# Second-product weights loaded through ScalarE's queue

## What is computed

```python
def swiglu(x, w_in, w_out):
    gu = x @ w_in
    g, u = jnp.split(gu, 2, axis=-1)
    return (jax.nn.silu(g) * u) @ w_out

x = x + 0.5 * swiglu(rmsnorm(x, norm_ffn1), ffn1_w_in, ffn1_w_out)
...
x = x + 0.5 * swiglu(rmsnorm(x, norm_ffn2), ffn2_w_in, ffn2_w_out)
```

## Time and profile before

| | us |
|---|---|
| median of 3 runs | 2199.1 |
| the profiled execution | 2206.41 |
| its span, first to last instruction | 2204.5 |
| TensorE busy (9208 matmuls) | 2084.3, 95% |
| VectorE busy | 1389.5, 63% |
| GpSimd busy | 891.9, 40% |
| ScalarE busy | 744.9, 34% |
| granted TensorE clock, mean | 0.968 |

### The profile page before, as it was taken

One profiled execution on the slowest core, in us unless ns is written; L12 is line 12 of the kernel. 1 busy time (PEld: TensorE's weight loads), 2 busy tenths in 40 slices (PEclk: granted clock), 3 DMA queues, 4 the chain that ended last, 5 costly groups with the idle time before them and its releaser, 6 DMA issues. The chain is left out here.

```text
span 2204.5 us, 27577 instructions
## 1 busy us (share of the span) xinstructions
PE 2084.3 (95%) x9208; PEld 1692.4 (77%) x9208; DVE 1389.5 (63%) x1570; ACT 744.9 (34%) x1048; POOL 891.9 (40%) x604
## 2 busy tenths in 40 slices
PE   7899999978898899999999999998999999888997
PEld 6688888866777788888877768886888888666776
DVE  5888887855445625434755555457888888655444
ACT  5444444421113321221134444224444444321112
POOL 0344444446568412312211112351444444366664
PEclk8999999989999999999999999999999999999998
DMA  3334344587652311112111114331544444695541
GB/s 115 126 130 166 133 171 143 186 307 273 246 209 76 115 59 41 57 57 76 58 48 39 53 58 151 129 143 45 175 142 157 147 166 148 244 348 199 201 171 76
DMA packets 147910, 307.85 MB, mean 140 GB/s; under 512 B 14096, under 2 KB 28560, under 8 KB 147856
## 3 DMA queue, kind: packets, MB, share of 16 engines
q1 hardware_dynamic: 139648, 278.97, 36.5%
q10 hardware_dynamic: 8208, 28.21, 3.4%
HBM read 205.42 MB, written 101.71 MB: 139 GB/s over the span
## 5 line engine op out<-in xcount | busy, mean ns | idle before, releaser
L1493 DVE SCALAR_TENSOR_TENSOR x<-ps,x 128x512 f32<-128x512 f32 x336 | 231.8, 691 | 235.6 <-PE ps L589 232.7
L1839 POOL TENSOR_TENSOR w_lo<-stage,w_hi 128x1024 fp32r<-128x1024 f32 x55 | 145.1, 2638 | 423.6 <-ACT w_hi L928 423.6
L537 PE MATMUL ps<-a_hi,w_hi 128*128 128x512 f32 x752 | 252.9, 404 | 1.2 <-DVE a_lo L1787 0.7
L537 PE MATMUL ps<-a_hi,w_lo 128*128 128x512 f32 x752 | 242.4, 390 | 0.0
L537 PE MATMUL ps<-a_lo,w_hi 128*128 128x512 f32 x752 | 242.3, 389 | 0.0
L1854 POOL TENSOR_TENSOR gb<-gb,rstd 128x512 f32<-128x512 f32 x42 | 89.4, 2130 | 353.4 <-DVE gb L1414 353.4
L1899 POOL TENSOR_TENSOR lo<-st,hi 128x1024 fp32r<-128x1024 f32 (+1 forms) x92 | 178.1, 1958 | 41.9 <-ACT hi L1029 41.9
L1029 ACT ACTIVATE hi<-st 128x1024 fp32r<-128x1024 f32 (+1 forms) x48 | 47.4, 988 | 386.8 <-POOL st L1890 256.4
L589 PE MATMUL ps<-a_hi,hi 128*128 128x512 f32 x264 | 113.1, 428 | 59.5 <-POOL lo L1899 37.9
L537 PEld LDWEIGHTS ps<-a_hi,w_lo 128*128 128x128 f32 x752 | 141.2, 188 | 29.8
L537 PEld LDWEIGHTS ps<-a_lo,w_hi 128*128 128x128 f32 x752 | 141.4, 188 | 29.4
(11 more groups left out here) (268 smaller groups left out, 4772.8 us busy)
## 6 DMA issues: line engine op xcount, KB each, us to landing
stage<-wstream SPq DMA_DIRECT2D x56, 512.0 KB, 3.3
b_spill<-raw_lo SPq DMA_DIRECT2D x110, 256.0 KB, 2.6
b_spill<-bh_a SPq DMA_DIRECT2D x88, 256.0 KB, 4.2
st_a<-win SPq DMA_DIRECT2D x42, 512.0 KB, 3.9
st_b<-win SPq DMA_DIRECT2D x42, 512.0 KB, 4.5
st<-wout SPq DMA_DIRECT2D x80, 256.0 KB, 3.9
b_spill<-bh_b SPq DMA_DIRECT2D x66, 256.0 KB, 4.0
t_hi<-b_spill SPq DMA_DIRECT2D x24, 512.0 KB, 10.1
```

Source lines behind the costliest of these rows:

```text
L537: mm = pe.matmul(ps[:, bank, :], w[0:r, k, :], mv[0:r, k, HALF * half:HALF * half + HALF], start=first and part == 0, stop=final and part ...
L1493: dve.scalar_tensor_tensor(out=x[:, m, part], in0=ps[:, bank, :], scalar=0.5, in1=x[:, m, part], op0=ALU.mult, op1=ALU.add).then_inc(xacc, 1)
L1839: pool.tensor_tensor(w_lo[:, parity, :, :], stage[:, parity, :, :], f32(w_hi[:, parity, :, :]), ALU.subtract).then_inc(wlo_done, 1)
```

## The change

`load_w2` moves from SyncE's program into ScalarE's, and is issued by ScalarE's queue. A helper `next_w2(f, s)` waits for the low part of pass s and then loads pass s + 2; it stands behind `high2(f, s)` for each s from 2 to 21. The pair of pass 0 stands in front of `high2(f, 0)` in the last `pair_in`; that of pass 1 behind the last silu, and right behind it that of pass 2; that of pass 3 stands behind the last `rest_combos`, in front of `high2(f, 2)`.

```diff
--- before.py
+++ after.py
@@ -411,19 +411,6 @@
                                  b_spill[qs[0]:qs[-1] + 1, NPROD * h + r, :, :].rearrange("q p n -> p q n")
                                  ).then_inc(cmb_first[r] if c == 0 else cmb_loaded[CMB_OF[c]], 16)
 
-            def load_w2(f, s):
-                b = s % 2
-                if s >= 2:
-                    sp.wait_ge(lo2_done, 2 * (NS * f + s - 1))
-                if kt_of(s) == 1:
-                    src = wodd[4 * f + s % 4, :, :].rearrange("p (s n) -> p s n", s=4)
-                    dst = st2[b][:, :, 0, :]
-                else:
-                    src = wout[(NS - 4) * f + (s if s < 4 else s - 4), :, :].rearrange("p (s n) -> p s n", s=4)
-                    dst = st2[b].rearrange("p s k n -> p s (k n)")
-                sp.dma_start(dst[:, 0:2, :], src[:, 0:2, :]).then_inc(w2_loaded[b], 16)
-                sp.dma_start(dst[:, 4:7:2, :], src[:, 2:4, :]).then_inc(w2_loaded[b], 16)
-
             def ffn(f):
                 J0, S0 = NP * f, NS * f
                 sp.wait_ge(lo1, 4 * J0 + 2)
@@ -445,21 +432,14 @@
                 last = J0 + NP
                 for r in range(NPROD):
                     sp.wait_ge(prod1, NPROD * (last - 1) + r + 1)
-                    if r == 6:
-                        load_w2(f, 1)
                     load_combo(f, 0, r, *CHUNKS[0])
                     if r == 1:
                         sp.wait_ge(c11_done, last)
                         reload_x(f, 1)
-                    if r == 3:
-                        load_w2(f, 0)
-                load_w2(f, 2)
                 sp.wait_ge(b1_done, last)
                 for m in (2, 6):
                     reload_x(f, m)
                 for r in range(NPROD):
-                    if r == 4:
-                        load_w2(f, 3)
                     load_combo(f, 1, r, *CHUNKS[1])
                 store_rest(f, (None, NQ - 1))
                 for r in (0, 2, 4, 1, 5):
@@ -468,13 +448,9 @@
                     reload_x(f, m)
                 for r in range(NPROD):
                     load_combo(f, 2, r, CHUNKS[2][0][:1], CHUNKS[2][1][:1])
-                load_w2(f, 4)
-                load_w2(f, 5)
                 for r in range(NPROD):
                     sp.wait_ge(prod2, NPROD * (S0 + 3) + r + 1)
                     load_combo(f, 2, r, CHUNKS[2][0][1:], CHUNKS[2][1][1:])
-                for s in range(6, 10):
-                    load_w2(f, s)
                 for c in range(3, len(CHUNKS)):
                     for r in range(NPROD):
                         sp.wait_ge(prod2, NPROD * (S0 + 4 * c - 5) + r + 1)
@@ -484,10 +460,6 @@
                         else:
                             load_combo(f, c, r, qs[:1], ks[:1])
                             load_combo(f, c, r, qs[1:], ks[1:])
-                    for s in range(4 * c - 2, 4 * c + 2):
-                        load_w2(f, s)
-                load_w2(f, NS - 2)
-                load_w2(f, NS - 1)
 
             load_w(U_TAIL1, 1, first=True)
             load_x(XO[0])
@@ -1016,6 +988,21 @@
                     act.wait_ge(b_stored[r], was_stored(Q, r, 0))
                     combo_high(r)
 
+            def load_w2(f, s):
+                b = s % 2
+                if kt_of(s) == 1:
+                    src = wodd[4 * f + s % 4, :, :].rearrange("p (s n) -> p s n", s=4)
+                    dst = st2[b][:, :, 0, :]
+                else:
+                    src = wout[(NS - 4) * f + (s if s < 4 else s - 4), :, :].rearrange("p (s n) -> p s n", s=4)
+                    dst = st2[b].rearrange("p s k n -> p s (k n)")
+                act.dma_start(dst[:, 0:2, :], src[:, 0:2, :]).then_inc(w2_loaded[b], 16)
+                act.dma_start(dst[:, 4:7:2, :], src[:, 2:4, :]).then_inc(w2_loaded[b], 16)
+
+            def next_w2(f, s):
+                act.wait_ge(lo2_done, 2 * (NS * f + s + 1))
+                load_w2(f, s + 2)
+
             def high2(f, s):
                 b, S = s % 2, NS * f + s
                 kt = kt_of(s)
@@ -1051,6 +1038,8 @@
                 if more:
                     next_weights(J, 1)
                 else:
+                    load_w2(last_of, 0)
+                if not more:
                     high2(last_of, 0)
                 silu_second(J)
 
@@ -1067,12 +1056,16 @@
                 last = NP * (f + 1)
                 J, Q = (None, last), (None, NQ * (f + 1) - 1)
                 silu_first(J)
+                load_w2(f, 1)
+                next_w2(f, 0)
                 rest_combos(J, Q, 0)
                 high2(f, 1)
                 rest_combos(J, Q, 1)
                 rest_combos(J, Q, 2)
+                next_w2(f, 1)
                 for s in range(2, NS - 2):
                     high2(f, s)
+                    next_w2(f, s)
                 end = NPROD * NS * (f + 1)
                 high2(f, NS - 2)
                 for t in range(2):
```

## The result

| | before | after |
|---|---|---|
| median, us | 2200.02 (4 runs) | 2148.92 (4 runs) |
| ratio, 95% interval | | 0.9771 (0.9754 to 0.9788) |
| span of the profiled run | 2204.5 | 2146.7 |
| its granted TensorE clock | 0.968 | 0.983 |

The change takes 51.1 us off. 2144 was predicted, with a range of 2130 to 2165: a gain of 55.4 us, 4.3 more than came.

The account below looks back on a forecast made before the run. TensorE was busy 95% of the span, so only its idle and low-clock time could be won. Gaps 53.6 plus start 1.8 make 55.4 us: 2206.4 to 2151.0 profiled, 2144 us for the median, range 2130 to 2165.

Parts of the forecast that it names:

- Part 1, the gaps: Before passes 4, 10, 14 and 18 of both blocks: earlier issue by ScalarE closes all eight gaps, gaining 53.6 us.
- The length of a pair in a backlog: Two `wout` loads on ScalarE's queue beside SyncE's backlog: 4.1 us for packets plus 2.3 latency, 6.4 us a pair.
- Part 2, the start: Passes 0 to 2: GpSimd starts 1.8 us earlier, two ScalarE issues cost 0.9; net gain 0.9 a block, 1.8 both.
- Part 3 and 4: ScalarE's 96 issues at 0.45 us, 43 us, fit its idle time; SyncE's freed queue wins nothing.
- signs of being right: No L1899 wait over 1 us from pass 3, passes 9.53 and 6.1, clock 1.00, pairs 5 to 7, pass 2 within 2.
- signs of being wrong: Pairs at 13 us or more, ScalarE issues above 1.5, GpSimd idle before pass 10, TensorE waiting for chunk loads or x.
- The high end of the range: Whole kernel: both starts 6.7 us later, 2159, plus a third of ScalarE's price: 2165 us.
- ScalarE's price: Slow issues on ScalarE, up to 2.51 us each, make passes late: some 18 us a block lost.
- A starved queue: Rival, at the start: pairs take up to 26 us beside SyncE's full queue, gaps stay, 2230 us; 5%.
- ScalarE pays for the issue: Rival, ScalarE's passes: issues up to 2.51 us each lose some 18 us a block, 2181 us; 7%.
- Nothing lands sooner: Rival, pairs in the backlog: they land behind it whoever issues, gaps stay, 0.9 us a block added, 2201 us; 3%.

Follow-up runs that it names:

- e8: Kernel before, with only the pairs from pass 4 on moved to ScalarE's queue, pairs 0 to 3 left on SyncE's: 2146.9 us, 0.9762.
- e1: Kernel before, all loads still in SyncE's queue, pairs for passes 4, 10, 14 and 18 moved ahead among the chunk loads: 2160.6 us, 0.9828.
- e2: Changed kernel, pairs for passes 10, 14 and 18 issued on ScalarE's queue about 7 us later than they could be: 2165.8 us, 0.9856.
- e5: Changed kernel, SyncE holds back all but the first of chunk 0's seven combinations until pass 0's pair has landed: 2147.6 us, 0.9757.
- e10: Changed kernel once more, unedited, run as a repeat on the same chip as a later version: 2153.0 us, 0.9778.

## Why the prediction was right, point by point

**Part 1, the gaps (53.6 us).** Right in mechanism and size: 26.52 + 27.12 = 53.6 us in passes 4 to 20. e8 shows that this part alone is the whole gain. e1 and e2 show that it has two halves: the time of issue, which alone all but closes the gaps before passes 10, 14 and 18, and the own queue, which alone narrows them. They overlap, and are not two sums to be added. The idle gap and the slow clock behind it were rightly priced together, by whole passes.

**The length of a pair in a backlog (6.4 us).** Too short. The pairs of passes 0 and 1 in the changed kernel, by ScalarE's issues and the first sums of VectorE and GpSimd:

```profile
448.66 0.60 ACT L974 ACTIVATE gb<-ps 128x512 f32<-128x512 f32 x1 [2.12 <-PE ps L561]
448.67 0.40 ACTq L999 DMA_DIRECT2D st<-wout  x1
...
464.74 0.34 ACTq L999 DMA_DIRECT2D st<-wout  x1
...
457.71 0.43 DVE L1441 TENSOR_TENSOR st<-st 128x256 f32<-128x256 f32 x1 [5.63 <-DMA st<-wout]
...
472.89 0.74 POOL L1880 TENSOR_TENSOR st<-st 128x256 f32<-128x256 f32 x1 [6.15 <-DMA st<-wout]
```

9.0 and 8.2 us. The pair of pass 10 took 9.8, here by ScalarE's issue and by GpSimd:

```profile
536.07 0.35 ACTq L999 DMA_DIRECT2D st<-wout  x1
...
545.88 0.74 POOL L1880 TENSOR_TENSOR st<-st 128x256 f32<-128x256 f32 x1 [2.16 <-DMA st<-wout]
```

The DMA view of the changed kernel shows what the model left out, for pass 0's pair, issued at 448.67. First from 448.67 to 452.25, then from 452.25 to 457.25:

```profile
q1 hardware_dynamic: 696, 1.34, 102.0%
```

```profile
q1 hardware_dynamic: 598, 1.40, 73.0%
q10 hardware_dynamic: 416, 0.52, 31.2%
```

In the first 3.6 us not one packet of ScalarE's queue was served. Then all 416 of the pair took 5.0 us, and VectorE began 0.5 us later. The model had 4.1 us for the packets, so one packet in turn was nearly right. The Trainium skill (DMA: Bandwidth & Descriptors, Queues, rings and completion order) says that a DMA engine goes round its queues packet by packet; the trace agrees, with 488 packets to 502 in e2. Too short was the fixed part: 2.3 us, where 3.6 + 0.5 passed. It came from loads alone on the wires, and there the first packet of a pair follows 1.0 us after the issue (677.23 and 678.2 in the kernel before). Why it takes 3.6 us beside a backlog stays open; e2 has 3.7 us for it (546.04 and 549.75), and e5, with hardly any backlog, 1.9. Besides, the 3.0 and 9.8 us that the prediction reads the earlier trace rows are medians of single transfers; the pairs took 3.5 us alone and 11.7 before pass 10. The error hardly mattered, as passes from 4 on had 13 us.

**Part 2, the start (a gain of 1.8 us).** This is the term that failed: it became a loss of 1.25 + 0.42 us. By its own formula, with two pairs of 9.0 and 8.2 us in the place of two of 6.4, GpSimd's first sum comes 2.6 us late and a forecast 1.8 - 0.9 = 0.9 a block turns into a loss of 3.5. It came out milder for three reasons. Pass 0's pair was issued with the start of the copy and not behind its end (448.67 for 449.3), and pass 1's with the start of the last silu (464.74 for 465.4), so GpSimd's first sum came 1.3 us late, counted from the copy, and not 2.6. The two issues cost about 0.5 us on ScalarE and not 0.9. And in f = 0 one of GpSimd's next sums (L1890, now L1883) took 0.73 us for 1.20, which no run explains.

**Part 3 and 4.** ScalarE's 96 issues took 0.33 to 0.73 us each, and from pass 3 on TensorE waited for no high half, as said. SyncE's freed queue gave nothing, as said.

**Not foreseen:** 0.74 us in passes 21 to 23 of f = 0 and 0.37 in pass 3 of f = 1, both of which the sum had at nothing. Their cause stays open; they are of the size by which one profile differs from the next (passes 21 to 23 of f = 0 take 37.2 us in e10, the same kernel).

**The signs.** Most signs of being right came: no wait for GpSimd's low line from pass 3 on, 9.52 and 6.1 us a pass, clock 1.00, pass 2 within 2 us of its place. One did not, the pair in 5 to 7 us. Two signs of being wrong came as well, both too small to matter: GpSimd stood idle for 2.2 us on a transfer of `wout` before pass 10, which TensorE did not feel, and TensorE waited 0.7 and 0.5 us for chunk 0's loads.

**The high end of the range.** It adds 6 us as a third of ScalarE's price. That price was 18 us a block, 36 in all, so a third is 12 us and the end 2171.

**The rivals.** A starved queue: no, 8 to 10 us and not 26. ScalarE pays for the issue: no. Nothing lands sooner: no. The Trainium skill's sentence that issuing from several engines saves only issue time (the same page, Issuing engines are not separate DMA queues) does not hold here as it stands. An earlier issue is worth three quarters of the gain, by e1, but e2 shows that the own queue saves more than issue time: 8.1 for 11.7 us at the same moment of issue.

## What to carry to other kernels

When a small load is late, look at two times apart: when its place was free and when it was issued, and then how long it took against its length alone. Here 7.6 us were its place in a hand-written queue, which moving one line in the same queue mends, and some more was the backlog, which only another queue or another order mends. And do not price a wait by its length: the one before pass 0 could be halved for nothing, because pass 1's pair was then issued too late, behind the last silu. Where it was issued behind the last product (e4), the blocks took 7.6 us less.

## What the runs showed that was not expected

ScalarE issues a transfer while its previous activation still runs: L974 starts at 448.66 and takes 0.60 us, and the issue starts at 448.67. So two issues between dependent activations cost about 0.5 us, not 0.9. In the changed kernel the high part of pass 2 starts 1.00 us after the start of the combination in front of it:

```profile
487.75 0.64 ACT L952 ACTIVATE bh_b<-t_raw 128x512 fp32r<-128x512 f32 x1 [1.07 <-POOL t_raw L1863]
487.75 0.33 ACTq L999 DMA_DIRECT2D st<-wout  x1
488.12 0.45 ACTq L1000 DMA_DIRECT2D st<-wout  x1
488.75 1.06 ACT L1016 ACTIVATE hi<-st 128x1024 fp32r<-128x1024 f32 x1 [0.37 <-issue]
```

Without them, in the kernel before, it starts 0.54 us after (492.46 and 491.92). And a separate queue does not free a load from a backlog: a pair of 512 KB takes 3.5 us alone, 4.4 with hardly any backlog (e5), 8.1 to 9.8 in one on its own queue (12.5 for pass 2's, issued right behind another pair), 11.7 to 12.9 in the same queue as the backlog.
